# State-space projections as three float32r products with split weights, low parts kept in the weight ring

## What is computed

```python
def mamba2_mixer(h, w_in, conv_w, conv_b, dt_bias, a_log, d_skip, norm_w, w_out):
    z, xbc, dt = split_cols(h @ w_in, SSM_SPLITS)        # 2048, 3072 and 32 columns
    xbc = causal_depthwise_conv(xbc, conv_w) + conv_b    # 4 taps
    xs_, Bm, Cm = split_cols(silu(xbc), (2048, 512, 512))
    dt = softplus(dt + dt_bias)
    ...                                                  # decays from cumsum(dt * A), state-space sums
    y = y * silu(z)
    y = rmsnorm(y per group of 512) * norm_w
    return y @ w_out                                     # 2048 x 1024
```

## Time and profile before

| | us |
|---|---|
| median of three runs | 2906.77 |
| runs | 2904.12 to 2908.88 |
| the profiled execution | 2906.48 |
| its span on the core | 2904.4 |
| input part, from project(1) to the last background step | 444.85 to 619.64 |
| decays and state sums | 619.64 to 659.34 |
| output part, slots 0 to 7 | 659.34 to 729.11 |

### The profile page before, as it was taken

One profiled execution on the slowest core, in us unless ns is written; L12 is line 12 of the kernel. 1 busy time (PEld: TensorE's weight loads), 2 busy tenths in 40 slices (PEclk: granted clock), 3 DMA queues, 4 the chain that ended last, 5 costly groups with the idle time before them and its releaser, 6 DMA issues.

```text
span 2904.4 us, 49935 instructions
## 1 busy us (share of the span) xinstructions
PE 2770.5 (95%) x22276; PEld 1973.9 (68%) x22276; DVE 1187.1 (41%) x2055; ACT 709.1 (24%) x1136; POOL 48.3 (2%) x39
## 2 busy tenths in 40 slices
PE   8899999999999999999998997999999999998998
PEld 6789997877433333333333765899999965687998
DVE  4667764241301101101111686355455533553554
ACT  2234333140200000000001115243334312211443
POOL 0000000000000000000000000000000000131000
PEclk9899999999999999999999999999999998999999
DMA  8756765544999999999999120256654430010552
GB/s 335 301 195 255 275 253 210 195 155 173 362 380 420 421 420 420 421 420 421 420 413 380 58 102 15 104 214 262 253 225 162 144 116 16 16 62 19 186 180 82
DMA packets 95198, 686.88 MB, mean 236 GB/s; under 512 B 10624, under 2 KB 11776, under 8 KB 11904
## 3 DMA queue, kind: packets, MB, share of 16 engines
q1 hardware_dynamic: 94400, 681.37, 59.4%
q10 hardware_dynamic: 576, 2.25, 0.2%
HBM read 682.52 MB, written 1.05 MB: 235 GB/s over the span
## 4 chain that ended last, share of the span: by engine, by line
PE 85%; DMA 7%; DVE 5%; ACT 2%; issue 1%; SPq 0%; POOL 0%; ACTq 0%; DVEq 0%
PE ps L526 42%; PE ps L2049 14%; PE ps L886 12%; PE ps L797 6%; PE ps L2074 5%; DMA AR<-W 3%; DMA ring<-W 2%; PE ps L539 2%; PE ps L2077 2%; PE ps L772 1%; PE ps L2057 1%; DVE macc L642 0%; SPq L3571 0%; DMA XT<-XIN 0%; DMA sml<-SM 0%
## 5 line engine op out<-in xcount | busy, mean ns | idle before, releaser
L2049 PE MATMUL ps<-AR 128*32 128x512 f32 x2904 | 441.1, 595 | 11.4 <-DMA AR<-W 9.7
L526 PE MATMUL ps<-HT,ring 128*128 128x256 f32 (+1 forms) x1696 | 441.9, 421 | 2.7 <-ACT HT L715 2.7
L526 PEld LDWEIGHTS ps<-HT,ring 128*128 128x128 f32 x1696 | 322.9, 192 | 114.8 <-issue 75.1
L526 PE MATMUL ps<-FR,FR 128*128 128x256 f32 x3120 | 388.6, 284 | 0.0
L526 PEld LDWEIGHTS ps<-FR,FR 128*128 128x128 f32 x3120 | 378.5, 192 | 7.9 <-issue 7.8
L868 DVE TENSOR_TENSOR FR<-ring,FR 128x2048 fp32r<-128x2048 f32 x129 | 294.4, 2290 | 145.8 <-ACT FR L852 145.7
L886 PE MATMUL ps<-FR,FR 128*128 128x256 f32 x2832 | 349.3, 283 | 0.0
L886 PEld LDWEIGHTS ps<-FR,FR 128*128 128x128 f32 x2832 | 343.9, 192 | 0.4 <-issue 0.4
L2169 DVE TENSOR_TENSOR AR<-AR,ps 128x256 f32<-128x256 f32 x70 | 29.6, 423 | 678.8 <-ACT AR L2132 361.0
L2049 PE MATMUL ps<-ring,AR 128*32 128x512 f32 x1576 | 288.1, 593 | 5.8 <-DMA ring<-W 3.5
L2049 PEld LDWEIGHTS ps<-AR 128*32 128x32 f32 x2904 | 121.8, 110 | 228.1 <-issue 226.3
(11 more groups left out here) (430 smaller groups left out, 2517.8 us busy)
## 6 DMA issues: line engine op xcount, KB each, us to landing
ring<-W SPq DMA_DIRECT2D x431, 1024.0 KB, 6.4
AR<-W SPq DMA_DIRECT2D x215, 1024.0 KB, 21.5
XT<-XIN ACTq DMA_DIRECT2D x2, 1024.0 KB, 8.5
cst<-CS SPq DMA_DIRECT2D x1, 1859.0 KB, 15.8
out<-XT SPq DMA_DIRECT2D x4, 256.0 KB, 2.2
sml<-SM SPq DMA_DIRECT2D x1, 970.5 KB, 11.9
cst<-CS ACTq DMA_DIRECT2D x1, 129.5 KB, 7.7
sml<-SM ACTq DMA_DIRECT2D x1, 16.0 KB, 5.3
```

The lines of the kernel that those rows point to most:

```text
L526: ins = g.matmul(out, l, r, **kw)
L2049: ins = g.matmul(bank.ap[group(i), :], mo.hg[e % 2][:, 4 * h + k, group(t)], w[n][:, k, :], start=j == 0 and k == 0, stop=j == 1 and k == ...
```

## The change

Nineteen input slots (2 to 20) and six output slots (2 to 7) are computed as three float32r products; input slots 0 and 1 and output slots 0 and 1 stay as they were. Per slot ACT makes the high part (128x2048) in a buffer of its own (`in_high`, `out_high`), and DVE overwrites the slot in the ring with the low part (`low`). So the ring place stays taken until PE is through with the slot, as before. The activations are split too: HT into `ma.hh` and `ma.hl` once, y in three groups of four tiles into `ma.yh` and `ma.yl`. In the input part ACT and DVE split slot n+2 at the start of their iteration n. In the output part DVE's copies for the background steps, until now all behind `gated(3)`, are put between the splits.

```diff
+        def split_act(g, s, n):
+            i = slot("ssm_in", n)
+            hi, last = in_high(n)
+            wait_slot(s, i)
+            if last >= 2:
+                s.wait_ge("ma.in", last)
+            g.activation(hi, flat(i), ACT.Copy).then_inc(*s.done("ma.wh", n))
+
+        def split_dve(g, s, n):
+            i = slot("ssm_in", n)
+            wait_slot(s, i)
+            s.wait_ge("ma.wh", n)
+            g.tensor_tensor(low(i), flat(i), in_high(n)[0].bitcast(F32), SUB).then_inc(*s.done("ma.wl", n))
...
 (project, n >= 2)
+                    s.wait_ge("ma.hl").wait_ge("ma.wl", n)
+                    w = [v.rearrange("p (k c) -> p k c", k=8) for v in (in_high(n)[0], low(i))]
+                    for h in range(2):
+                        ins = mm(g, b.ap[:, h * 256:h * 256 + 256], [p for k in range(8) for p in three(...)])
...
 (mamba_act)
             for n in range(1, 13):
                 ps = counts.bank("ma.in", n)
+                split_act(g, s, n + 2)
                 s.wait_ge("ma.in", n)
...
             root_act(g, s, "ma.rms3", 13, 2, 512)
+            s.wait_ge("ma.y_ps", 15)
+            split_out_act(g, s, 2)
+            y_high_act(g, s, 1)
+            split_out_act(g, s, 3)
+            split_out_act(g, s, 4)
+            y_high_act(g, s, 2)
+            split_out_act(g, s, 5)
+            split_out_act(g, s, 6)
+            y_high_act(g, s, 3)
+            split_out_act(g, s, 7)
...
 (mamba_dve)
             for n in range(1, 21):
+                if n < 19:
+                    split_dve(g, s, n + 2)
                 if n == 2:
...
             for q in range(4):
                 gated(q)
-            bg.go(6)
+            y_low_dve(g, s, 1)
+            split_out_dve(g, s, 2)
+            bg.go()
+            split_out_dve(g, s, 3)
+            for n, q in ((4, 2), (5, None), (6, 3), (7, None)):
+                split_out_dve(g, s, n)
+                if q:
+                    y_low_dve(g, s, q)
+                bg.go()
+            bg.go()
```

More of the change, by code:

```diff
@@ L444, in sb, with twice @@
             return ctx.enter_context(nc.sbuf_tensor(name, shape, dt))
+        def twice(name, shape):
+            with ExitStack() as c:
+                plain = c.enter_context(nc.sbuf_tensor(name, shape, F32))
+            return plain, sb(name + "R", shape, F32R)
         co, ncst = offsets(CONST)
         so, nsm = offsets(SMALL)
-        ring = sb("ring", [128, RING, SLOT])
+        ring, ringR = twice("ring", [128, RING, SLOT])
         cst = sb("cst", [128, ncst])
@@ L451, in program @@
         XT = sb("XT", [128, 2, 8, 256])
-        HT = sb("HT", [128, 8, 512])
+        HT, HTr = twice("HT", [128, 8, 512])
         SC, SC2 = sb("SC", [128, 8]), sb("SC2", [128, 8, 32])
@@ L499, in flat, with low @@
             return ring[:, place, :] if place < RING else more[:, place - RING, :]
+        def low(i):
+            return ringR[:, where[i][0], :]
         def by8(i):
@@ L515, in memory, with over @@
                 return Memory(nc, c, n, *a)
+        def over(n, at, *sizes):
+            with ExitStack() as c:
+                if at:
+                    c.enter_context(nc.sbuf_tensor(f"GAP{n}", [128, at], F32))
+                return [c.enter_context(nc.sbuf_tensor(f"OV{n}_{i}", [128, k], F32R))[:, :] for i, k in enumerate(sizes)]
         ident, ones, eps, one = cs("ident"), cs("ones"), cs("eps"), cs("ones", 0, 1)
@@ L801, in down_slot, with down_slot3 @@
             ins.then_inc(*s.done("down", x, i, frees=(sl,) if free else ()))
+        def down_slot3(g, s, x, i, n, acc, sl, w, rhs, ready):
+            w = [v.rearrange("p (k c) -> p k c", k=2) for v in w]
+            for one_ready in ready:
+                s.wait_ge(*one_ready)
+            for kk, m in down_order(i == n - 1):
+                k, h = 2 * i + kk, m % 2
+                for j, (l, r) in enumerate(three([v[:, kk, m * 128:m * 128 + 128] for v in w], rhs(k))):
+                    ins = g.matmul(acc[m // 2].ap[:, h * 256:h * 256 + 256], l, r, start=False, stop=k == 2 * n - 1 and h == 1 and j == 2,
+                                   skip_group_check=True)
+                if i == n - 1 and kk == 1 and m in (1, 3, 5):
+                    ins.then_inc(*s.done("two", x, m // 2))
+            ins.then_inc(*s.done("down", x, i, frees=(sl,)))
         def down_end(x):
@@ L1558, in program, with in_high, out_high, split_out_act @@
         ma.y = ma.cv[:, 0:16, :]
+        ma.early = over(31, 12312, SLOT, SLOT)
+        ma.wide = over(32, 19192, SLOT, SLOT, 2048)
+        ma.hh, ma.hl = HTr[:, :, 256:512], ma.wide[2].rearrange("p (k t) -> p k t", k=8)
+        ma.vh = over(33, 10240, SLOT, SLOT, SLOT)
+        ma.yh = over(34, 0, 4096)[0].rearrange("p (k t) -> p k t", k=16)
+        ma.yl = over(35, 4096 + 4 * 256, 3072)[0].rearrange("p (k t) -> p k t", k=12)
+        def in_high(n):
+            if n < 10:
+                return (ma.wide[0], ma.wide[1], ma.early[0], ma.early[1])[(n - 2) % 4], n - 4
+            return ma.wide[n % 2], n - 4 if n < 12 else n - 2
+        def out_high(i):
+            return ma.vh[i % 3]
+        def split_act(g, s, n):
[10 more added lines that the diff above has]
+            g.tensor_tensor(low(i), flat(i), in_high(n)[0].bitcast(F32), SUB).then_inc(*s.done("ma.wl", n))
+        def split_out_act(g, s, n):
+            i = slot("ssm_out", n)
+            wait_slot(s, i)
+            if n >= 5:
+                s.wait_ge("down", "ma.down", n - 3)
+            g.activation(out_high(n), flat(i), ACT.Copy).then_inc(*s.done("ma.vh", n))
+        def split_out_dve(g, s, n):
+            i = slot("ssm_out", n)
+            wait_slot(s, i)
+            s.wait_ge("ma.vh", n)
+            g.tensor_tensor(low(i), flat(i), out_high(n).bitcast(F32), SUB).then_inc(*s.done("ma.vl", n))
+        def y_high_act(g, s, q):
+            s.wait_ge("ma.g", 4 * q + 3)
+            g.activation(ma.yh[:, 4 * q:4 * q + 4, :], ma.y[:, 4 * q:4 * q + 4, :], ACT.Copy).then_inc(*s.done("ma.yh", q))
+        def y_low_dve(g, s, q):
+            k = slice(4 * q, 4 * q + 4)
+            s.wait_ge("ma.yh", q)
+            g.tensor_tensor(ma.yl[:, 4 * q - 4:4 * q, :], ma.y[:, k, :], ma.yh[:, k, :].bitcast(F32), SUB).then_inc(*s.done("ma.yl", q))
         def conv_tiles(n):
@@ L1572, in project @@
                 s.wait_emptied(b)
-                wait_slot(s, i)
-                for h in range(2):
-                    ins = proj(g, i, h * 128, 128, b.ap[:, h * 256:h * 256 + 256], 0, 256)
+                if n == 1:
+                    wait_slot(s, i)
+                    for h in range(2):
+                        ins = proj(g, i, h * 128, 128, b.ap[:, h * 256:h * 256 + 256], 0, 256)
+                else:
+                    s.wait_ge("ma.hl").wait_ge("ma.wl", n)
+                    w = [v.rearrange("p (k c) -> p k c", k=8) for v in (in_high(n)[0], low(i))]
+                    for h in range(2):
+                        ins = mm(g, b.ap[:, h * 256:h * 256 + 256], [p for k in range(8) for p in three([v[:, k, h * 128:h * 128 + 128] for v in w],
+                                                                                                     [ma.hh[:, k, :], ma.hl[:, k, :]])])
                 ins.then_inc(*s.done("ma.in", n, frees=(i,)))
@@ L1694, in mamba_pe @@
                     spread(3)
-                down_slot(g, s, "ma.down", "ssm_out", i, 8, acc, lambda k: ma.y[:, k, :], [("ma.g", 2 * i + 1)])
+                if i < 2:
+                    down_slot(g, s, "ma.down", "ssm_out", i, 8, acc, lambda k: ma.y[:, k, :], [("ma.g", 2 * i + 1)])
+                else:
+                    sl = slot("ssm_out", i)
+                    down_slot3(g, s, "ma.down", i, 8, acc, sl, (out_high(i), low(sl)), lambda k: (ma.yh[:, k, :], ma.yl[:, k - 4, :]),
+                               [("ma.vl", i), ("ma.yl", i // 2)])
                 bg.go((1, 0, 1, 1, 1, 1, 1, 0)[i])
@@ L1704, in mamba_act @@
             s.wait_marks("dn.end")
+            s.own().activation(ma.hh, HT[:, :, 0:256], ACT.Copy).then_inc(*s.done("ma.hh"))
+            split_act(g, s, 2)
             def silu(n):
@@ L1774, in mamba_dve @@
             g.memset(ma.raw[:, :, 0:3], 0.0).then_inc(*s.done("ma.pad"))
+            s.wait_ge("ma.hh")
+            g.tensor_tensor(ma.hl, HT[:, :, 0:256], ma.hh.bitcast(F32), SUB).then_inc(*s.done("ma.hl"))
+            split_dve(g, s, 2)
             for n in range(1, 21):
+                if n < 19:
+                    split_dve(g, s, n + 2)
                 if n == 2:
```

## The result

The change makes the kernel slower: 2918.0 us (median of five runs, 2917.6 to 2919.2) against 2906.8 us for the kernel before, measured with it, a ratio of 1.0039 with a 95% interval of 1.0028 to 1.0050. The profiled execution has a span of 2915.6 us, 11.2 us more than that of before.

What follows compares the result with a forecast made beforehand. PE, busy 95% of the span, was taken as the bound. Input -4.7 us and output +17.4 us, waits and clock included, gave +12.7 us on 2906.5, so 2919.2 us; range 2906 to 2938.

Steps and rivals of the forecast that it cites:

- The slot: 16 float32 products (7.01 us) become 48 float32r ones: 5.83 us per input slot; input and output slots together save 29.9 us.
- (d): Rival: products run at the float32 passes' gap, 109.5 ns, saving 12 us more, 2907 us; chance 0.03.
- Place 1: Input part, n == 4: softplus and `ma.av` stand behind slot 6's split on DVE; PE waits 9.2 us.
- Place 2: Input part, cb: `ma.nc` stands behind slot 11's split on DVE; PE waits 5.6 us, 3.1 us more than before.
- Place 3: Start of output slot 2: low y stands behind gated(3) on DVE, then slot 2's split; PE begins 5.4 us later.
- Place 4: Output background steps behind slots 3, 4, 5: DVE's copy stands behind the next split; waits 5.1, 3.9, 5.1, sum 14.1 us.
- The clock: Granted clock falls after long PE waits: 2.7 us charged four times, 10.8 us; bounds 0 and twice that.
- (a): Rival: the output part hides its chain, freeing to copy under 5.8 us, so places 3 and 4 cost nothing; 2894 us; chance 0.11.
- (c): Rival: loads fall behind at two per 7.26 us step, copies come late and waits grow; 2938 us; chance 0.15.
- (b): Rival: the clock stays up after the waits, so its 10.8 us are not lost; 2908.4 us; chance 0.13.

Runs made afterwards that it cites:

- cum_late: The change, but PE sums the decays behind project(5) instead of project(4); 2914.9 us.
- nc_early: The change, but DVE makes `ma.nc` in iteration 8, right behind the split of slot 10, not in iteration 9; 2913.5 us.
- warm: The change, but PE fills its wait for `ma.av` with 66 products that are thrown away; 2918.4 us.
- out_free: The change with output part reordered: background steps behind slots 0 to 5, slot 2's halves made earlier, DVE's copies before the splits that follow; 2894.8 us.
- all_last: all_free, with DVE's split of slot n+2 moved to the end of its input iteration n; 2879.6 us, ratio 0.9910 to the kernel before.
- out_only: The change with only the 6 output slots split, input part left in float32; 2930.0 us, ratio 1.0080 to the kernel before.
- all_free: out_free with the moves of cum_late and nc_early added; 2881.3 us, ratio 0.9916 to the kernel before.

## Why the prediction was right

2919 us was forecast, 2918.0 measured, and the terms stand up one by one.

- **The slot.** Forecast 5.83 us, measured 5.77 (461.44 to 467.21). It has the pace of the dense layer, where weight loads are busy for 163.6 of 165.0 us; the rival (d) at the pace of float32 passes is out. That the weight loads set this pace is read from that busy share; no run tested it. The rule of the Trainium skill that was named with it (TensorE: Matmul & The Clock Gate, section Back-to-back issue gap, N/2.4 + 2.5 ns) would make this slot 5.2 us; the trace does not agree, 5.77 us for 48 products are 120 ns each. The prediction should have said that the section gives this formula for an isolated matmul, and states that in a stream of weight loads and matmuls both set the spacing.
- **Place 1.** Forecast a wait of 9.2 us, measured 8.6; slot 6 landed 6.9 us after the start of project(4), 0.5 us earlier than the 7.4 of the forecast, and `ma.av` came 15.8 us after it in place of 16.4. The run cum_late shows that the account of who waits behind it was incomplete.
- **Place 2.** Forecast 5.6, measured 5.4 us; nc_early took it away with its clock (6.8 us in the part).
- **Place 3.** Forecast 5.4 us later. Measured 5.2 (from the start of output slot 0 to that of slot 2, 20.6 us before and 25.9 after), of which 5.1 are the wait.
- **Place 4.** Forecast 5.1, 3.9 and 5.1 us, measured 4.9, 3.2 and 3.3. The chain is right to 0.2 us. The second and third waits are shorter because the slots in front of them ran at half clock for part of their time and filled the wait: from 697.50 to 706.83, where PE was ready, are 9.3 us for a step of 7.2, and 9.0 us in the next. I had seen that for slot 4 only. The sum for the output part, +17.7 measured against +17.4, owes its closeness in part to luck: the background step behind slot 3 itself ran at half clock (2.8 us in place of 1.4, 697.50 to 700.31), and as its end frees the place of slot 5, it put 1.4 us on the chain where the forecast charged nothing. The clock in slot 2 cost 1.4 us less than charged, and the two cancel.
- **The clock.** Charged four times 2.7 us. Measured 2.5 (place 1, by the run warm), 2.2 behind cb (522.69 to 532.06, 9.4 us for 7.2), 1.3 in slot 2 (678.14 to 685.25, 7.1 us for 5.8) and 3.1 behind slot 5 (10.3 us for 7.2): 9.1 in place of 10.8, besides the 1.4 us above. What the clock cost at places 1 and 2, the slot's 0.06 us nineteen times and the two waits came to 2.6 us less than forecast; project(1) took 0.25 us more (7.26 us in place of 7.01). Together that is the 2.4 us by which the input part came out better.
- **Rivals.** (a), that the output part hides its chain, failed where I said it would: 10.7 us from the freeing to the copy against 5.8. (c), loads behind, was not seen: the loads of input slots 4 to 10 landed 6.8 to 8.1 us after their issue, PE's list has no wait for a low part in the input part, and in out_free and all_last the step of 7.2 us holds. (d) is answered under the slot. (b), a clock that stays up, is out by the windows above.

What no run settles is the part of the time outside the layer: it varies by several us from kernel to kernel with no edit in it, and the errors of my experiments' totals in out_only, nc_early and all_last are of that size. The median came within 1.2 us of the forecast, which is closer than that spread lets a sum of such terms promise.

## What to carry to other kernels

A cheaper product on the bound engine is paid out only if the preparation that it needs does not stand, in another engine's fixed order, ahead of something else that the bound engine wants; list for each split what is queued behind it and when that is wanted, the small copies too. Where the ring is short, the time from the freeing of a place to what the bound engine wants from behind the landing (here 10.7 us: load, two passes, copy) must be over when it wants it. In the change PE wanted it one slot, 5.8 us, behind the step that freed the place; in out_free it is two whole steps (for slot 5 14.3 us, from 684.49 to 698.80 in its trace), because each place is freed a step earlier, in the order of the loads. The same 25 slots cost 11 us or won 26 us by order alone.

## What the runs showed of the hardware

Whether the clock falls after an idle time of some 3.4 us is not fixed. The wait of 3.50 us ahead of the first products of this layer is the same in all kernels and ends in the same way. Before, the clock stayed at 1.00 behind it; in the change it was down in the same window:

```profile
441.00:445.00 4.00, 3.58 (x16) 1.32 (x16) 2.54 (x8) 3.91 (x9) 0.00 (x0) 0.66 0.02 4
```

In the traces of the twelve kernels (before, the change and ten runs) it was down behind this wait in seven. It cost little there: from the end of the wait to that of project(1) are 10.95 us in the change and 10.26 before, 0.7 us more. A wait of 3.42 us in cum_late was followed by 0.50 for longer:

```profile
485.50:489.00 3.50, 3.50 (x24) 2.21 (x24) 3.50 (x7) 1.03 (x3) 0.00 (x0) 0.50 0.21 87
489.00:493.00 4.00, 4.00 (x20) 4.00 (x20) 3.69 (x8) 0.00 (x0) 0.00 (x0) 0.50 0.74 266
```

It cost 4.4 us, and one of 3.44 us in all_free at the same place 3.1 us (486.26 to 498.00, 11.7 us for the same 8.6). I had taken to say that 3.5 us are harmless and 4.2 are not. The traces say that a wait of this length costs between 0 and 4.4 us; what decides it they do not show. A fall in one kernel and not in the next can be part of why untouched stretches differ.
